# Score products of a chunked bidirectional scan, made in column tiles of 32 and 64 instead of full 128 by 128 products

## The reference, cut to what matters

```python
scores = jnp.einsum("bhtk,bhsk,bhtsk->bhts", qc, kc, decay)      # decay: products of f between s and t
o = o_inter + jnp.einsum("bhts,bhsv->bhtv", scores, vc)
s_new = jnp.exp(last)[..., None] * s + jnp.einsum("bhsk,bhsv->bhkv", kc * jnp.exp(last - cum), vc)
```

## Time and profile before

| what | value |
|---|---|
| median of 3 runs | 2581.43 us (2580.27 to 2581.68) |
| span of the profiled execution | 2581.9 us |
| TensorE matmuls, weight loads | 97%, 81% of the span |
| VectorE, GpSimd, ScalarE | 72%, 50%, 45% |
| mean granted clock of TensorE | 0.991 |
| HBM traffic | 258.58 MB read, 90.70 MB written |

### The profile page before, as it was taken

How to read it: one execution, slowest core, us unless ns; L and a number is a source line. 1 busy time by engine, 2 the same in 40 slices (tenths; PEclk the granted TensorE clock), 3 DMA queues, 4 the chain that set the end, 5 groups by cost and what they waited for, 6 DMA issues and landing times.

```text
span 2581.9 us, 35674 instructions
## 1 busy us (share of the span) xinstructions
PE 2510.4 (97%) x12344; PEld 2094.9 (81%) x12344; DVE 1860.8 (72%) x2441; ACT 1156.6 (45%) x2159; POOL 1299.2 (50%) x859
## 2 busy tenths in 40 slices
PE   8999999999999989999999999999999999999998
PEld 6888888888887778888888877877887888888886
DVE  5377778767856476888877988888656565556898
ACT  4344534544443453333344467333454433434544
POOL 3112321431330037777877972678304767766983
PEclk8999999999999999999999999999999999999999
DMA  6123422432352343444458342032514322345533
GB/s 262 57 79 135 180 104 101 152 126 74 131 216 111 130 141 116 155 138 167 162 184 309 117 127 86 33 131 98 196 57 148 113 99 94 122 171 216 188 99 114
DMA packets 124249, 351.14 MB, mean 136 GB/s; under 512 B 12752, under 2 KB 12752, under 8 KB 121040
## 3 DMA queue, kind: packets, MB, share of 16 engines
q1 hardware_dynamic: 124112, 349.33, 38.6%
HBM read 258.58 MB, written 90.70 MB: 135 GB/s over the span
## 4 chain that ended last, share of the span: by engine, by line
PE 81%; DVE 8%; POOL 3%; issue 3%; ACT 3%; DMA 2%; SPq 1%; DVEq 0%; ACTq 0%; POOLq 0%
PE psum L1538 18%; PE psum L1540 18%; PE psum L1539 18%; PE psum L2125 4%; PE psum L2127 4%; PE psum L2126 4%; PE psum L1798 2%; PE psum L1800 2%; PE psum L1799 2%; PE psum L1750 2%; POOL row_unit_sum L1454 1%; PE psum L1737 1%; PE psum L1764 1%; PE psum L1720 1%; DVE k_all L3266 1%
## 5 line engine op out<-in xcount | busy, mean ns | idle before, releaser
L1538 PE MATMUL psum<-x_hi,unit 128*128 128x512 f32 x1232 | 483.8, 393 | 8.2 <-DVE x_lo L2967 7.7
L1540 PE MATMUL psum<-x_hi,unit 128*128 128x512 f32 x1232 | 480.2, 390 | 0.0
L1539 PE MATMUL psum<-x_lo,unit 128*128 128x512 f32 x1232 | 480.2, 390 | 0.0
L2967 DVE TENSOR_TENSOR c_set<-c_set,psum 128x512 f32<-128x512 f32 x352 | 233.1, 683 | 221.9 <-ACT c_set L2249 146.6
L1403 POOL TENSOR_TENSOR unit<-unit_sum,unit 128x512 fp32r<-128x512 f32 x200 | 291.9, 1467 | 14.1 <-ACT unit L2249 12.2
L1538 PEld LDWEIGHTS psum<-x_hi,unit 128*128 128x128 f32 x1232 | 231.8, 188 | 63.7 <-ACT c_set L2249 5.7
L1540 PEld LDWEIGHTS psum<-x_hi,unit 128*128 128x128 f32 x1232 | 231.5, 188 | 48.5
L1539 PEld LDWEIGHTS psum<-x_lo,unit 128*128 128x128 f32 x1232 | 231.8, 188 | 47.0
L1538 PE MATMUL psum<-h_hi,w_hi 128*128 128x512 f32 x624 | 262.6, 421 | 0.2 <-DVE h_lo L2967 0.2
L2125 PE MATMUL psum<-row_unit_hi,part_hi 128*128 128x512 f32 x616 | 241.9, 393 | 3.0 <-DVE part_lo L2967 1.8
L1540 PE MATMUL psum<-h_hi,w_lo 128*128 128x512 f32 x624 | 244.2, 391 | 0.0
(11 more groups left out here) (353 smaller groups left out, 5801.1 us busy)
## 6 DMA issues: line engine op xcount, KB each, us to landing
ffn_raw<-in_w_ffn_in SPq DMA_DIRECT2D x80, 512.0 KB, 5.9
part_raw<-parts_kept SPq DMA_DIRECT2D x154, 256.0 KB, 2.7
parts_kept<-part_sums SPq DMA_DIRECT2D x22, 1280.0 KB, 5.5
ada_half<-in_ada SPq DMA_DIRECT2D x96, 256.0 KB, 2.6
out_raw<-in_w_ffn_out SPq DMA_DIRECT2D x44, 512.0 KB, 7.5
w_raw<-in_w_hgrn_in SPq DMA_DIRECT2D x40, 512.0 KB, 3.6
ada_raw<-in_ada SPq DMA_DIRECT2D x32, 512.0 KB, 4.9
units_kept<-stage_unit SPq DMA_DIRECT2D x28, 512.0 KB, 2.9
```

Source lines behind the costliest of these rows:

```text
L1538: begin = pe.matmul(out_ap, hi[:, a:b], rhs_hi, start=first, stop=False)
L1539: pe.matmul(out_ap, hi[:, a:b], rhs_lo, start=False, stop=False)
L1540: return begin, pe.matmul(out_ap, lo[:, a:b], rhs_hi, start=False, stop=last)
L2967: V.tensor_tensor(dst, a, b, op).then_inc(S[sem], 1)
```

## The change

`near` and `level` no longer make one product of 128 keys by 128 queries for a chunk. `score_width` gives a width: 32 for `near` and for levels 3 and 4, 64 for levels 5 and 6. For a chunk there are then 128 / width products, each of `width` keys by `width` queries over all 128 channels. Product s takes the keys s of the chunk and writes to the PSUM partitions from s * width on, with `tile_position=(0, s * width)`: a column tile of the array. For `near` and levels 3 to 5 the queries are those of the same positions, so that only the blocks on the diagonal are made; for the last level they are those of the other half, read straight from the direction's own tensor. What else stands in the bank is left from earlier uses, and the readers, which are as before, pick none of it. The semaphores, their counts, the banks and the order of the calls stay.

```diff
--- before.py
+++ after.py
@@ -826,12 +826,12 @@

             return ap.rearrange("p (n two b) -> p n two b", two=2, b=b)

-        def both(t, first, b):
-
-
-            one = t[:, 0, first:first + P]
+        def both(t, first, b, n=P):
+
+
+            one = t[:, 0, first:first + n]
             width = t.shape[2]
-            pattern = [list(one.ap[0]), [2 * b, P // (2 * b)], [width + b, 2], [1, b]]
+            pattern = [list(one.ap[0]), [2 * b, n // (2 * b)], [width + b, 2], [1, b]]
             return bass.AP(tensor=one.tensor, offset=one.offset, ap=pattern)


@@ -1727,28 +1727,49 @@
                     pe.wait_ge(S["ctx_evac"], hh * 3 + (1 + 3))
                 transposes(hh, U_V + part, v_t, range(4 * part, min(4 * part + 4, CHUNKS)))

+            def score_block(b, c, width, keys, queries):
+
+                first = b * HALF + c % 4 * P + queries * width
+                return psum[keys * width:(keys + 1) * width, first:first + width]
+
+            def score_width(i):
+                return P // 4 if i < NEAR + 2 else GRID_W
+
             def near(hh, part, last):

+                width = score_width(0)
                 for d in (FWD, BWD):
                     pe.wait_ge(S["near_copied"], hh * 4 + 2 * (d + 1))
                     pe.wait_ge(S["near_scaled"], hh * 4 + 2 * (d + 1))
                     b = scan_use(hh, U_NEAR + 2 * part + d)
                     for c in range(4 * part, 4 * part + 4):
-                        mm = pe.matmul(bank(b, (c % 4) * P, (c % 4 + 1) * P), chunk(near_keys(d), c),
-                                       chunk(near_queries(d, last), c), start=True, stop=True)
+                        for s in range(P // width):
+                            own = slice(c * P + s * width, c * P + (s + 1) * width)
+                            mm = pe.matmul(score_block(b, c, width, s, s), near_keys(d)[:, own],
+                                           near_queries(d, last)[:, own], start=True, stop=True,
+                                           tile_position=(0, s * width))
                     mm.then_inc(S["scan_full"], 1)
                     yield

             def level(hh, i, part):


+                width = score_width(i)
                 b = scan_use(hh, far_use(i, part))
                 pe.wait_ge(S["k_merged"], hh * 4 * len(FAR_LEVELS) + 2 * (2 * (i - NEAR) + part) + 2)
                 for d in (FWD, BWD):
                     pe.wait_ge(scan_sem[d], hh * SCAN_STEPS + queries_decayed(i - 1, part))
                 for c in range(4 * part, 4 * part + 4):
-                    mm = pe.matmul(bank(b, (c % 4) * P, (c % 4 + 1) * P), chunk(k_both, c),
-                                   both(q_all, c * P, 1 << i), start=True, stop=True)
+                    for s in range(P // width):
+                        first = c * P + s * width
+                        keys = k_both[:, first:first + width]
+                        if i < LAST:
+                            mm = pe.matmul(score_block(b, c, width, s, s), keys, both(q_all, first, 1 << i, width),
+                                           start=True, stop=True, tile_position=(0, s * width))
+                        else:
+                            other = c * P + (1 - s) * width
+                            mm = pe.matmul(score_block(b, c, width, s, 1 - s), keys, qd[s][:, other:other + width],
+                                           start=True, stop=True, tile_position=(0, s * width))
                 mm.then_inc(S["scan_full"], 1)

             def key_transposes(hh, d, part):
```

## The result

The changed kernel takes 2558.98 us (median of 4 runs, 2555.89 to 2561.32) against 2581.55 us of the kernel before (4 runs). The ratio is 0.9911, 95% interval [0.9897, 0.9925]: it is 0.9% faster, 23 us, where 2619 us and a slower kernel were forecast. The wider range of 2548 to 2715 holds it only because it was drawn around that rival too.

A forecast was written before the change was run, and what follows sets the result against it. TensorE's dense stream was taken to bound the heads; 6.4 + 0.3 for passes and 30.7 for borders, +37.4 us on 2581.9, gave 2619 us; own range 2588 to 2655, wider range with rivals 2548 to 2715.

The forecast's parts named there:

- that rival: Score calls: column tiles work beside each other, so it gets faster, 2543 us without borders to 2574 with them; chance 0.25.
- The bound, and one to one: Heads: a TensorE stream with hardly a hole, matmuls covering 97% of the span; changes to TensorE's time count one to one.
- the wait ahead of level 6: Before line 1750, 5.3 us in seven waits: a round trip through ScalarE's key copies behind q, neither swallowing nor returning time.
- What a call costs now, and why: Near and level score calls: 0.89 us each, 111 ns a pass, set by loading 128 weight columns; 96 calls, 85.5 us.
- The price of a pass on one tile: Tiled score calls: 31 ns for a 32-column pass, 56 for a 64-column one.
- as long as passes follow one another: Tiled score calls: passes run in sequence, 0.99 us a 32-wide call and 0.90 a 64-wide one, +6.4 and +0.3 us.
- The borders: Switches between full-width and tiled work around each call: emptying the array costs 0.32 us a call, +30.7 us in all.
- Instructions as the bound, the second rival: Tiled score calls: instruction pace limits TensorE, 2653 us at 43 ns each, 2714 at 56; chance 0.20.
- VectorE's slack: Heads: VectorE waits for line 1750, 3.44 us at a head's first level, so it has slack.

## Why the prediction was wrong, step by step

**The bound, and one to one: right.** TensorE's calls shrink by 21.8 us and the span by 22.3, or by 2.7 and 2.5 in one head; everything behind the last call is as long as it was. The reading of the wait ahead of level 6 was right too, as the run with the copies moved shows.

**What a call costs now, and why: right as far as it went.** A call took 0.89 us, and the row with one streamed column shows that loading 128 columns in every pass set that.

**The price of a pass on one tile: right.** I took 31 ns for 32 columns and 56 for 64; one tile takes a pass in 32 and 62.

**The step that failed: "as long as passes follow one another".** I took 32 x 31 ns for a call, as though the array had one tile. Passes start 8.5 ns apart on four tiles, so the term measured 0.26 us and not 0.99, and on two tiles of 64 it measured 0.46 and not 0.90. The run with one tile, which is the world that I forecast, takes 2622 us where I said 2619. The trace of before had no tiled work, so the rows could only give the pace of one tile. I wrote the other case down as a rival, and gave it 0.25, where the rows spoke for neither.

**The rival was right in kind and too timid in size.** I let the second pass of a product wait 31 ns on its tile before the next product began, and had 0.50 us for 32-wide calls. By the single records four passes start within some 20 ns and each next four 32 ns behind (53 the first time), so both passes of a product overlap with those of three others: 0.26 us. For 64-wide calls I had 0.45, and 0.46 was measured. With borders of 0.33 and 0.35 us that makes 0.59 and 0.81 us a call, and 2560 us; with my 0.82 and 0.77 it was 2574.

**The borders: right in size.** I took 0.32 us more than the passes; 0.33 was measured, 0.35 where they were doubled. The rule of the Trainium skill, TensorEngine Tiling (Array Packing), Key Properties, that a change of tiling mode drains TensorE, agrees with this: 0.13 us between tiles of 32 and tiles of 64 in one call, while a change of tile costs 6 to 8 ns. The same skill's figure for matmuls of different tiles, some 4 ns apart (TensorE: Matmul & The Clock Gate, Part 3), is close to the 6 to 8 ns between starts here; its sentence in that part that loads overlap running matmuls only where row groups differ does not hold here, since 32 loads for column tiles, which share their row groups, run for 0.35 us from 154.02 beside the 32 matmuls that start there.

**Instructions as the bound, the second rival: wrong.** 64 loads and matmuls of a call start within 0.26 us, 4 ns each; the 56 ns were only the pace of the loads. The larger queue brought 14 packets more, 98 and not 84, where I had estimated 12, and the waits on "issue" ahead of the near calls went from 0.9 to 1.1 us.

**VectorE's slack: right for the change, wrong for more of it.** It shows 1.3 us of new waits for the near picks, and takes back nearly all of the gain where near calls come closer together.

## What to carry to other kernels

Small products that use a part of the array's columns gain from column tiles only if neighbouring instructions go to different tiles: four tiles take 8.5 ns a pass, one tile 32, four products in a row on the same tile 23. Going from full-width to tiled work costs some 0.1 us here and coming back 0.24, so a call must hold enough passes to pay 0.33 us: 32-wide calls gain 0.30 us each and 64-wide ones 0.08. And an engine named behind a wait is a guess of the profile: here it had been done for a third of a microsecond before the wait ended, and the order of another engine's queue was the cause.

## What was not expected of the hardware

A 32-column pass lasts 196 ns from start to end and yet 32 of them fit between two dense matmuls 0.71 us apart. The pace of a tile of 32 is 32 ns whether one, two or four are at work. Going from tiles of 32 to tiles of 64 costs 0.13 us at the change, as much as lies between the last tiled matmul of a 32-wide call and the first dense one.
